# A routed mixture of experts on one core: where the scatter of an expert's results stands in the code, and how many slot channels it multiplies

## The reference, cut to what matters

```
logits = tok @ w_router + b_router
top_p, top_i = lax.top_k(softmax(logits), 2)
gates = (one-hot of top_i, times top_p / sum(top_p))        # 256 x 8
out = 0
for e in range(8):
    out = out + gates[:, e:e+1] * swiglu(tok, w_gate_up[e], w_down[e])
...
swiglu(h, wgu, wd):  gate, up = split(h @ wgu);  (silu(gate) * up) @ wd    # d_ff = 3584
```

## Time and profile before

| what | value |
|---|---|
| median of 3 runs | 1817.26 us (1816.25 to 1817.8) |
| profiled execution, its own time | 1811.8 us |
| its span, first to last instruction | 1810.1 us |
| PE busy | 1503.2 us, 83% |
| DVE, ACT busy | 718.9 us, 520.6 us |
| mean granted TensorE clock | 0.933 |
| weights and inputs read | 471.47 MB |
| matmul records of L1743 (scatter) | 136: eight before the loop, 16 in each of the eight iterations |

### The profile page before, as it was taken

How to read it: one execution, slowest core, us unless ns; L and a number is a source line. 1 busy time by engine, 2 the same in 40 slices (tenths; PEclk the granted TensorE clock), 3 DMA queues, 4 the chain that set the end, 5 groups by cost and what they waited for, 6 DMA issues and landing times.

```text
span 1810.1 us, 26654 instructions
## 1 busy us (share of the span) xinstructions
PE 1503.2 (83%) x11310; PEld 1058.3 (58%) x11311; DVE 718.9 (40%) x770; ACT 520.6 (29%) x645; POOL 71.7 (4%) x72
## 2 busy tenths in 40 slices
PE   2678869999979887899989997576699975887786
PEld 1545437888868445677767774243467753544443
DVE  6397444444420444666556651010067710100102
ACT  1222233343320332555445550010156500101001
POOL 0043210000010001000000000000000000000000
PEclk9899979999989996899999998878799987899999
DMA  8879823555524211377647776999999959999993
GB/s 297 297 267 330 331 94 140 186 186 186 186 103 173 97 36 58 141 278 279 234 179 270 269 262 229 393 391 394 394 393 379 361 209 392 393 394 394 384 393 118
DMA packets 206826, 474.83 MB, mean 262 GB/s; under 512 B 9987, under 2 KB 10031, under 8 KB 206671
## 3 DMA queue, kind: packets, MB, share of 16 engines
q1 hardware_dynamic: 199968, 470.83, 70.5%
q10 hardware_dynamic: 6702, 1.71, 0.5%
HBM read 471.47 MB, written 1.05 MB: 261 GB/s over the span
## 4 chain that ended last, share of the span: by engine, by line
PE 66%; SPq 16%; DMA 5%; issue 4%; ACT 4%; DVE 4%; ACTq 1%; POOL 1%; DVEq 0%
PE ps L1566 31%; SPq L368 16%; DMA ring<-in_moe_w_down_dram 5%; PE ps L1637 3%; PE ps L1888 3%; PE ps L1797 3%; PE ps L1743 2%; PE ps L1453 2%; PE ps L1723 2%; PE ps L1854 2%; PE ps L1731 2%; PE ps L1536 2%; PE ps L1702 2%; PE ps L1551 2%; PE ps L1645 2%
## 5 line engine op out<-in xcount | busy, mean ns | idle before, releaser
L1356 DVE TENSOR_TENSOR ring_lo<-ring,w 128x2048 fp32r<-128x2048 f32 x119 | 272.5, 2291 | 132.1 <-ACT w L790 116.7
L790 ACT ACTIVATE w<-ring 128x2048 fp32r<-128x2048 f32 x119 | 227.6, 1915 | 192.8 <-PE ps L1566 177.1
L1797 PE MATMUL ps<-ring,arena 128*32 128x128 f32 (+1 forms) x3584 | 211.3, 340 | 78.0 <-DMA ring<-in_moe_w_gate_up_dram 70.9
L1797 PEld LDWEIGHTS ps<-ring,arena 128*32 128x32 f32 (+1 forms) x3584 | 155.8, 133 | 144.5 <-issue 76.1
L1566 PE MATMUL ps<-ring_lo,x_hi 128*128 128x512 f32 x532 | 208.5, 392 | 0.0
L1331 DVE TENSOR_TENSOR arena<-arena,ps 128x128 f32<-128x128 f32 (+1 forms) x35 | 11.9, 341 | 385.1 <-PE ps L1797 385.1
L1854 PE MATMUL ps<-ring,arena 128*32 128x512 f32 (+1 forms) x560 | 105.5, 702 | 38.3 <-DMA ring<-in_moe_w_down_dram 38.3
L753 ACT ACTIVATE arena<-ps 128x128 f32<-128x128 f32 (+1 forms) x35 | 11.2, 320 | 433.6 <-PE ps L1797 433.6
L1566 PE MATMUL ps<-w,x_hi 128*128 128x512 f32 x308 | 127.2, 413 | 2.5 <-DVE ring_lo L1356 2.5
L1566 PE MATMUL ps<-w,x_lo 128*128 128x512 f32 x308 | 120.9, 393 | 0.0
L1093 DVE TENSOR_TENSOR ring_lo<-ring,w_hi 128x2048 fp32r<-128x2048 f32 x42 | 95.6, 2290 | 61.9 <-ACT w_hi L623 61.9
(11 more groups left out here) (305 smaller groups left out, 2086.1 us busy)
## 6 DMA issues: line engine op xcount, KB each, us to landing
ring<-in_moe_w_gate_up_dram SPq DMA_DIRECT2D x112, 2048.0 KB, 17.3
ring<-in_moe_w_down_dram SPq DMA_DIRECT2D x56, 2048.0 KB, 18.9
ring<-in_ada_w_dram SPq DMA_DIRECT2D x24, 2048.0 KB, 12.1
ring<-in_ffn_w_gate_up_dram SPq DMA_DIRECT2D x14, 2048.0 KB, 8.1
ring<-in_ffn_w_down_dram SPq DMA_DIRECT2D x7, 2048.0 KB, 7.7
ring<-in_sb_w_qkv_dram SPq DMA_DIRECT2D x6, 2048.0 KB, 7.9
ring<-in_s_w_out_dram SPq DMA_DIRECT2D x2, 2048.0 KB, 9.1
ring<-in_sb_w_out_dram SPq DMA_DIRECT2D x2, 2048.0 KB, 7.9
```

The costliest lines, as they stand in the source:

```text
L790: act.activation(half3(h).bitcast(F32R), ff_half(gran(N_MOE + g), half), ACT.Copy).then_inc(whi_done, 2 if g in plain else 1)
L1356: dve.tensor_tensor(ff_half(ring_lo[(N_MOE + g) % RING][:, :], half).bitcast(F32R), ff_half(gran(N_MOE + g), half), half3(h), ALU.subtract ...
L1797: ins = pe.matmul(ps[width * r:width * r + width, bank, 0:cols], x[:, k, 0:width], weights[:, k, cols * r:cols * r + cols], start=k == 0, ...
```

## The change

Each body calls `scatter` itself, before its branch to the shared code. `narrow` with one pass and `whole(False)` scatter channel 0 alone (4 matmuls, 8 records); `whole(True)` and `narrow` with two passes scatter both. The shared code is left with the back edge alone.

```
                             if f:
                                 down_product(f - 1, ch, width)
+                    scatter(e + 1, len(passes))

                 def whole(tail):
...
                         if g == down_at(FB - 2):
                             turn_main(FB - 1)
                             gather(e + 1, True)
+                    scatter(e + 1, 2 if tail else 1)

                 by_kind(whole, narrow)
-                scatter(e + 1)
             gate_row(3)
```

## The result

The changed kernel takes 1844.5 us (median of 4 runs, 1840.68 to 1848.45) against 1816.76 us for the kernel before (4 runs): a ratio of 1.0153, with an interval of 1.013 to 1.0175. It is slower by 27.7 us. The forecast (1831.7 us) had the direction and, as will be seen, the places, but a loss of 14.4 us.

A forecast was written before the change was run, and what follows sets the result against it. The sequencer's branches were taken to bound the transitions between experts. The terms 5.7 + 5.6 + 4.4 + 1.0 + 1.0 - 3.3 summed to +14.4 us, forecasting 1831.7 us, range 1819 to 1840 us.

The forecast's parts named there:

- What bounds the transitions: Between experts, the sequencer's branches set the time to the next expert's first product; the scatter lies beside them.
- Rival 4: Scatter is on the path: experts 3, 4 and 7 give 3.55 us each, expert 6 1.1; 1805.5 us, chance 0.04.
- rival 3: Branch at the body's end costs nothing in its new place, sequencer still bounds: -4.65 us, 1812.6 us, chance 0.06.
- Half the scatter: At the ends of experts 2 to 6 halving gives 0; only the very end gains, -3.3 us.
- the term of 1.0 us for the clock: Expert 3 to 4: PE's gap grows from 2.9 to 6.4 us, the clock may fall; +1.0 us, between 0 and 2.
- The branch at a body's end: Now behind scatter's wait: costs 3.3 to 3.8 us at experts 0, 1, 4, 7 and 6.29 at expert 6.
- Rival 2: A granule still loading makes branch and back edge slow at experts 1 and 4: +25.6 us, 1842.9 us, chance 0.08.
- The back edge behind the branch: Behind a body's branch it follows in a row, ending 3.4 to 3.5 us later, 6.0 under full DMA.
- Rival 1: Only the branch is exposed, the back edge takes its 0.46 us: sum +2.1 us, 1819.4 us, chance 0.12.
- Expert 1: Expert 0 to 1: sequencer 5.7 us later, mostly covered by PE's scatter and DVE; +1.0 us, between 0 and 5.7.
- Experts 6 and 7: Expert 6 to 7: branch 6.3 and back edge 6.0 us after the copies, on the path; +4.4 us.

The follow-up runs named there:

- the first shifted kernel: The changed kernel with two more matmuls in the body for over 160 tokens, which no expert takes: 1838.74 us, ratio 1.0131.

## Why the prediction was wrong in size

*What bounds the transitions.* Right. The sequencer's branches set them and not the scatter: the move with full scatters has nearly the whole loss. Rival 4 falls with that, and rival 3 with branches of 3.3 to 6.6 us in their new place.

*Half the scatter.* Right: it gives at the end alone, 3.4 us of 3.3 forecast, and 3.5 us in the kernel that halves without moving. In expert 4's stretch the term of 1.0 us for the clock measured 1.5; the first product there took 1.7 us longer.

*The branch at a body's end.* This is the step that failed, as a term that was mis-sized: "It costs 3.79, 3.29, 3.49 and 3.47 us where DMA is idle or light (experts 0, 1, 4, 7)". These rows stand where the branch stood before, at a moment when DMA was idle. The move also put it behind the release of the last granule, which starts a load. It cost 6.02, 6.03 and 6.60 us, and holding that load back brought 3.82, 3.31 and 3.33 us. Rival 2 named this mechanism and priced the back edge behind it at 6.0 us too; measured from the branch's end the back edge ended after 3.1, 3.5 and 3.4 us, as the forecast had it, for the load ended 1.3 to 1.4 us behind the branch at experts 1 and 4. That rival 2's time, 1842.9 us, lies 1.6 us from the measured one is chance: it had both steps at 12.3 us, where they took 9.5 and 10.0, and nothing for the code's place. So each of experts 2 and 5 gets about 2.7 to 3.1 us more than forecast from the branch. The next far branch, L341, gave 1.4 us of it back: 3.75 us instead of the 5.13 it took before, a term that I had left out. It is the same effect the other way round: before, a load was in flight until 1098.4 us while this branch lasted from 1093.8 to 1098.9; after the change DMA stands still from 1105.3 us on, and the branch comes at 1109.9.

*The code's place.* Not in the prediction at all: 3.1 us at the start of the body of width 32, in experts 2 and 5. Shifting code that never runs took them away. For expert 2 the sum is then 5.7 + 2.7 - 1.4 + 3.1 = 10.1 us, and 10.7 were measured; for expert 5 it is 5.6 + 3.1 - 1.4 + 3.1 = 10.4, and 10.1 were measured. From the scatter to PE's first record alone the two grew by 10.0 us (13.9 to 23.8) and 10.2 us (14.1 to 24.3).

*The back edge behind the branch.* Right: both stand in a row. Rival 1, with 0.46 us, falls with four rows of 2.9 to 5.8 us. The single packets show why it was short before: at experts 0 and 1 its 16 KB packet started at 904.4 and 1088.6 us, while the sequencer waited for the copies, and the back edge came at 905.6 and 1090.4 us. After the change the packet starts 0.6 us behind the start of the back edge.

*Expert 1.* 1.0 us forecast with the sequencer 5.7 us late; it was 7.5 us late and the stretch grew by 2.7. With the load held back the sequencer was 5.5 us late, and the stretch was 185.1 us, 0.3 more than before. The cover was as described, and the branch's price went through it.

*Experts 6 and 7.* 3.2 us of 4.4. The branch took 6.24 us and the back edge ended 6.0 us after it, as forecast.

The Trainium skill, "Advanced Engine Details and Errata", Control Flow Timing, has about 108 ns for a compare-and-branch. The rows show 0.26 us for the branch of the short test, whose target is near, and 3.3 to 7.6 us for those over a body. By the Trainium skill, "Runtime: NRT & Kernel Launch", Instruction fetch mechanics, a taken branch whose target is outside the two pages held waits until a page is fetched by DMA. The traces agree: each of the branches of experts 0, 1 and 4 has its packet, and with a load in flight that packet starts 2.0 to 3.1 us later.

What stays open: how the 27.7 us between the medians and the 24.1 us of the ledger divide between the executions' own spread and the kernel, and which placement effect lengthened the last branch in the first shifted kernel (two instruction packets moved during it, where the changed kernel's has one).

## What to carry to other kernels

In this kernel a branch over a long body is a transfer: price it by the load on DMA at the moment where it will stand, not where it stood. Keep it, and the back edge, in front of the wait that ends a body, so that the wait covers them; if a body's end needs a variant, put a short test into the shared code. Before trimming an engine's work at a loop's turn, look at whether its sequencer has gone past that work already, and after any change of code compare the first gaps of each body, for here a shift alone opened or closed gaps of 3.1 to 5.8 us.

## What the runs showed of the hardware

- PE's sequencer takes a whole scatter of 32 records (16 matmuls, 16 weight loads) into its queue and is at the back edge 0.2 us after the first of them has started.
- One 2 MB load in flight makes a far branch take 6.0 to 6.6 us instead of 3.3 to 3.8; its 16 KB instruction packet starts 3.5 to 4.1 us after the branch instead of 1.0 to 1.5, and the branch ends 1.4 us behind it.
- Right behind a far branch the hinted back edge ended 3.1 to 3.5 us after it with DMA idle or nearly so, 6 us under full DMA; without a far branch before it (experts 2, 3 and 5), it took 0.37 to 0.46 us.
- Two more matmuls in code that never runs took away three gaps of 3.1 to 5.8 us; ten more beyond these opened two of 4.8 and 4.7 us in another body.
